# A fused RWKV-7 block loop on one core: the key's square moves to ScalarE, the decay less its step to VectorE, and two queues are reordered

## The reference, cut to what matters

```
w_log = -softplus(-(w0 + tanh(wd) @ w_lora_up)) - 0.5
decay = exp(-exp(w_log))
a  = sigmoid(a0 + ad @ a_lora_up)
kk = k * k_k
kk = kk * rsqrt(sum(kk*kk, per head) + 1e-12)
k  = k * (1 + (a - 1) * k_a)
S_t = S_{t-1} diag(decay_t) + (S_{t-1} (-kk_t)) (kk_t * a_t)^T + v_t k_t^T
y_t = S_t r_t
```

## Time and profile before

| what | value |
|---|---|
| median of 3 runs | 2628.68 us (2628.33 to 2629.49) |
| profiled execution | 2628.31 us, its span 2626.6 us |
| granted TensorE clock, mean | 0.988 |
| PE busy | 2547.5 us, 97% of the span |
| DVE busy | 1520.5 us, 58% |
| ACT busy | 1163.3 us, 44% |
| POOL busy | 484.0 us, 18% |

### The profile page before, as it was taken

The page is one execution under the profiler, slowest core; times in us unless marked ns, Lnnn a source line. Parts: engine busy times, 40 slices in busy tenths (PEclk is TensorE's granted clock), DMA queues, the critical chain, the costliest instruction groups (busy, mean ns, idle before and its releaser), DMA issues.

```text
span 2626.6 us, 74898 instructions
## 1 busy us (share of the span) xinstructions
PE 2547.5 (97%) x30741; PEld 2102.5 (80%) x30741; DVE 1520.5 (58%) x3199; ACT 1163.3 (44%) x2626; POOL 484.0 (18%) x622
## 2 busy tenths in 40 slices
PE   6999999999999999999999999999999999999995
PEld 6777777777778888888888888888888888888883
DVE  2412121212157677777767777776677777667774
ACT  3324242323225455544445554454455445445542
POOL 3210101010121112211211121121112112111210
PEclk8999999999999999999999999999999999999997
DMA  8632322323210001000000101000010100001000
GB/s 338 255 112 81 110 93 99 102 90 112 81 65 10 26 29 39 26 34 26 26 26 26 42 26 34 26 26 26 26 42 26 34 26 26 26 26 42 26 18 25
DMA packets 68706, 153.08 MB, mean 58 GB/s; under 512 B 3977, under 2 KB 37342, under 8 KB 66398
## 3 DMA queue, kind: packets, MB, share of 16 engines
q1 hardware_dynamic: 63134, 130.08, 14.1%
q0 software_dynamic: 1680, 11.01, 1.0%
q10 hardware_dynamic: 3632, 7.87, 0.8%
HBM read 98.61 MB, written 50.33 MB: 57 GB/s over the span
## 4 chain that ended last, share of the span: by engine, by line
PE 74%; DVE 16%; ACT 4%; issue 3%; DMA 1%; DVEq 0%; SPq 0%; ACTq 0%
PE banks L949 20%; PE banks L355 16%; PE banks L984 9%; PE banks L387 8%; PE banks L932 7%; PE banks L1004 6%; DVE SM L1587 2%; DVE LA L1570 2%; DVE LA L1576 2%; PE banks L960 1%; PE banks L1112 1%; DVE t L1467 1%; DVE mix L1438 1%; DVE kk L1474 1%; DVE stmp L1519 1%
## 5 line engine op out<-in xcount | busy, mean ns | idle before, releaser
L949 PE MATMUL banks<-xT,w 128*128 128x128 f32 x5232 | 634.0, 279 | 0.0
L949 PEld LDWEIGHTS banks<-xT,w 128*128 128x128 f32 x5232 | 598.3, 192 | 31.1 <-issue 27.1
L1255 ACT ACTIVATE LX<-banks 128x512 f32<-128x512 f32 (+1 forms) x384 | 184.9, 524 | 642.6 <-DVE WT L1532 436.5
L355 PE MATMUL banks<-xT,w 128*128 128x256 f32 x2048 | 448.3, 381 | 4.8 <-ACT xT L475 4.8
L355 PEld LDWEIGHTS banks<-xT,w 128*128 128x128 f32 x2048 | 391.3, 191 | 65.3 <-issue 10.5
L932 PE MATMUL banks<-xT,w 128*64 128x128 f32 x6944 | 420.1, 274 | 0.0
L932 PEld LDWEIGHTS banks<-xT,w 128*64 128x64 f32 x6944 | 380.3, 137 | 6.3
L984 PE MATMUL banks<-wo,Y 128*128 128x512 f32 x512 | 234.3, 601 | 4.7 <-DVE Y L1492 4.7
L387 PE MATMUL banks<-wo,yc 128*128 128x512 f32 x512 | 224.8, 592 | 0.0
L672 DVE TENSOR_SCALAR gate<-gate 128x1024 f32<-128x1024 f32 x16 | 11.1, 694 | 367.7 <-ACT gate L495 367.7
L1532 DVE TENSOR_TENSOR WT<-banks,level_mask 128x256 f32<-128x256 f32 x256 | 102.6, 422 | 187.7 <-PE banks L1004 179.7
(11 more groups left out here) (185 smaller groups left out, 3587.6 us busy)
## 6 DMA issues: line engine op xcount, KB each, us to landing
x_in<-in_x SPq DMA_DIRECT2D x16, 1024.0 KB, 7.4
xr<-in_x SPq DMA_DIRECT2D x32, 512.0 KB, 4.3
xt_dram<-xT SPq DMA_DIRECT2D x32, 512.0 KB, 8.6
h_dram<-xr SPq DMA_DIRECT2D x32, 512.0 KB, 2.6
xT<-xt_dram SPq DMA_DIRECT2D x32, 512.0 KB, 3.3
gate_row<-h_dram SPq DMA_DIRECT2D x32, 512.0 KB, 4.3
out<-gate_row SPq DMA_DIRECT2D x32, 512.0 KB, 2.6
w<-in_w_in POOLq DMA_DIRECT2D x8, 1088.0 KB, 10.9
```

The source lines that it names most:

```text
L355: last = nc.tensor.matmul(bank[t // 2][:, (t % 2) * T1:(t % 2 + 1) * T1], w1[:, k, t * P:(t + 1) * P], xT[:, k, :], start=(k == 0), stop=( ...
L949: last = (by_halves if halves else nc.tensor.matmul)(bank[b][:, q * P:(q + 1) * P], w2[:, k, (t0 + q) * P:(t0 + q + 1) * P], xT[par][:, k, :],
L1255: s(nc.scalar.activation(to, of, ACT.Copy), lx_ready, hold=False)
```

## The change

Four things change, in the steady blocks and, the first two, in the prologue too.

1. The key's square leaves POOL (L1368) and becomes an ACT instruction, `key_square`, with function Square. In a block it stands behind `sigmoid(0)`, which itself moves ahead of `second_values(SV)`.
2. The subtraction for `egx` leaves POOL (L1370) and becomes a DVE instruction, `decay_ahead`, behind `take_r(1)` and ahead of `new_key`.
3. `state_sum(j)` waits for `s_ps` instead of `y_ps`. The wait for `y_ps` moves to `new_state(0)` and, for the second chunk, to the start of the next `run`.
4. DVE's order: `clamp(1)` goes between `state_sum(0)` and `new_state(0)`; `decay_sum` ahead of `take_r(1)`; the first two instructions of `replaced_key` (now `taken_key`) ahead of `shift(3)`, its last two (`decayed_key`) stay behind. ACT's order: `sigmoid(1)` ahead of `key_scale`.

```diff
 ACT:
+                def key_square():
+                    hd.wait(kk_ready, 1)
+                    hd(nc.scalar.activation(rn[:, :, :], kk[:, :, :], ACT.Square), kk2_ready, hold=False)
...
                     if ahead:
                         exp_low_rank(1)
+                        sigmoid(0)
+                        key_square()
                     s.wait(y_ps, 1)
                     second_values(SV)
...
                     if ahead:
-                        sigmoid(0)
+                        sigmoid(1)
                         key_scale()
-                        sigmoid(1)
                     take_u(1)
 POOL:
-                    hd.wait(kk_ready, 1)
-                    hd(nc.gpsimd.tensor_tensor(rn[:, :, :], kk[:, :, :], kk[:, :, :], ALU.mult), kk2_ready)
-                    hd.wait(G_ready, 1)
-                    hd(nc.gpsimd.tensor_tensor(egx[:, :, :], G[:, :, :], sig[:, 0], ALU.subtract), gprev_ready)
 DVE:
+                def decay_ahead():
+                    hd(nc.vector.tensor_tensor(egx[:, :, :], G[:, :, :], sig[:, 0], ALU.subtract), gprev_ready, hold=False)
...
-                def replaced_key():
+                def taken_key():
                     hd.wait(rn_ready, 1)
                     hd(nc.vector.tensor_tensor(kk[:, :, :], kk[:, :, :], rn[:, :, :], ALU.mult))
                     hd(nc.vector.scalar_tensor_tensor(out=t2[:, :, :], in0=kk[:, :, :], scalar=-1.0, in1=sig[:, 1],
                                                       op0=ALU.mult, op1=ALU.mult))
+
+                def decayed_key():
                     hd.wait(exps_ready, 1)
...
                 def state_sum(j):
-                    s.wait(y_ps, j + 1)
+                    s.wait(s_ps, j + 1)
...
                     if not first:
                         pv.block(n - 1)
+                        pv.wait(y_ps, NC)
...
                     state_sum(0)
+                    if ahead:
+                        clamp(1)
+                    s.wait(y_ps, 1)
                     new_state(0, s, s_ready)
                     if ahead:
-                        clamp(1)
+                        decay_sum()
                     take_r(1)
                     if ahead:
-                        decay_sum()
+                        decay_ahead()
                         new_key()
                     state_sum(1)
                     if ahead:
+                        taken_key()
                         shift(n + 1, 3)
-                        replaced_key()
+                        decayed_key()
```

## The result

| kernel | median, us | runs | ratio to before, 95% |
|---|---|---|---|
| before | 2628.8 | 4, 2628.33 to 2629.49 | |
| changed | 2611.45 | 4, 2610.13 to 2612.34 | 0.9931 [0.9918, 0.9944] |

The change saves 17.3 us, 0.7%. The profiled execution took 2610.13 us, its span 2608.4.

The account below looks back on a forecast made before the run. TensorE sets the pace, with a link through VectorE once per block. From 2628.31 us, 31 x 0.45 = 14.0 and 0.9 (last block) go, 0.9 of stalls comes back: 2614.3, stated as 2614.5; range for 8 in 10, 2604 to 2624.

Parts of the forecast that it names:

- What TensorE could win: Its waits for VectorE's LA and W at block start: at most 0.91 us in A, 0.56 in B.
- g: How much earlier VectorE gets to LA and W, decided between clamp and BK: about 0.45 us a block.
- A: Block kind where TensorE waits for LA and again for W: 0.48 and 0.43 us to win.
- B: The other, alternating block kind: 0.42 us to win at the wait for LA, 0.14 at W.
- The 0.2 us for POOL's copy of prev's column: End of VectorE's sequence: this copy now meets VectorE's BK and takes back up to 0.2 us.
- The hold of kk and t by BK: Behind state_sum(1), POOL's BK holds up VectorE's kk and t: together 2.4 to 2.6 us instead of 1.4.
- The first rival: BK and taken_key miss each other, no hold-up: g 1.6, TensorE's limits bind, 2605 us; chance 0.12.
- the largest step: State_sum(1) starts behind L1058, at about 1858.1 against 1859.57, 1.47 us earlier, allowed by s_ps rather than y_ps.
- ScalarE in the middle: Ln, Exp, Square and SV copies end just in time for TensorE: stall 0 to 0.2 us a block, taken 0.03.
- The margin of 0.2 us: Mid-block, ahead of L1034: ScalarE could be about 0.2 us later before TensorE's 0.03 us stall starts to grow.
- The prologue: Egx fills VectorE's idle time, the square moves between idle engines: 0, plus or minus 1 us.
- The last block: TensorE waits 2.04 us for new_state(0); with state_sum(0) not waiting for y_ps, 0.9 us is saved.

Follow-up runs that it names:

- e3: Changed kernel with POOL making only a 64x64 piece of each half of BK in the blocks: 2603.9 us in one run.
- e9: Changed kernel with kk ahead of k2, t ahead of state_sum(1), rk behind it, and the square first in ScalarE's prologue: 2601.98 us, ratio 0.9894.
- e7: Kernel before the change, with state_sum waiting for s_ps and the waits for y_ps moved accordingly: 2626.53 us, ratio 0.9992.
- e1: Changed kernel with state_sum waiting for y_ps again in both chunks: 2639.1 us, ratio 1.0035.
- e10: Changed kernel with state_sum(1) alone waiting for y_ps, state_sum(0) still for s_ps: 2618.31 us in one run.
- e8: Changed kernel with the key's square back on POOL, in the blocks and the prologue: 2617.25 us in one run.
- e6: Changed kernel with a second Square of 128x512 on ScalarE ahead of the key's square in each block: 2625.31 us in one run.
- e2: Changed kernel with the key's square ahead of the eight exponentials in ScalarE's prologue: 2608.21 us in one run.
- e5: Changed kernel with kk and t ahead of state_sum(1), rk behind it, and the square first in ScalarE's prologue: 2605.34 us, ratio 0.9913.
- e4: Changed kernel with the last shift ahead of kk and t again: 2619.26 us, ratio 0.9961.

## Why the prediction was right

Direction and mechanism held: 2611.45 against 2614.5, inside the range of 2604 to 2624. But three terms were off, and they partly cancelled.

*What TensorE could win and g.* Right in kind: the wait for LA is gone, the one for W in A is partly left. The size was too small: 0.70 us in A and 0.76 in B instead of 0.45, 22.4 us instead of 14.0 (of the 31 blocks 16 are of kind A and 15 of kind B, not the other way round as I counted; this makes the first rival's 22.6 a 23.0 and touches no other sum). One part is g. From L1058 to VectorE's BK it is 5.42 us now (1846.81 to 1852.23) and was 6.09 (1857.35 to 1863.44), so g is 0.67 and not 0.45. The 0.2 us for POOL's copy of prev's column was the wrong item: it starts 0.05 us ahead of BK and takes 0.22, and BK takes 1.43 against 1.41, so it holds nothing up. The other part is that L1112 can follow L1103 after 0.52 us; I had read 0.62 from the profile, which hid 0.1 us of wait. With my limit of 0.56 in B, the g of 0.67 would have been cut short there; the real limit is 0.64 (0.51 at LA and 0.13 at W). The remaining 0.07 us a block came between L1034 and the variance (3.95 to 3.90 and 6.66 to 6.64), which no step of mine foresaw and no run isolated.

*The hold of kk and t by BK.* This was the step I was least sure of. Kk and t take 2.38 us from start to end (1848.47 to 1850.85), at the low end of the forecast's 2.4 to 2.6. e3 shows that POOL's BK is the cause, e9 that who is issued first decides who waits. The rule of the Trainium skill that I weighed (SBUF — State Buffer, "Who interferes with whom") agrees, also in what it exempts: in e9 state_sum and the shift, with one input in PSUM, take 0.88 and 1.12 us beside BK. Only the end of the hold differs a little from the rule's whole length: the way is free about 0.14 us ahead of BK's recorded end. The first rival is what e3 shows, 2603.9 against 2605, but its limits were too low: the pair is 113.44 where they gave 113.73 (115.20 less 0.91 and 0.56). The 31 blocks are 27.0 us shorter than before in e3 instead of 22.6, and the later start of the second pass (2.7) and a last block that gained 0.1 instead of 1.9 hide that in the time.

*State_sum(1) and s_ps.* It starts 0.1 us behind the end of L1058, as forecast. But I called it the largest step and said that s_ps allows it. That was wrong as a statement of cause. In the kernel before, VectorE reached state_sum(1) when rk was done (1859.53), later than y_ps, so s_ps alone changes nothing (e7). It counts only in the new order, and there it is needed in both chunks (e1, e10). That what made room for it is POOL's two instructions gone, the shorter clamp and L1472 and the earlier sigmoid(1) is read from the rows; only the square has a run of its own (e8). I had not priced state_sum(0) at all, where it is worth more, 1.01 us of the pair.

*ScalarE in the middle.* The square ended at 1841.92 where TensorE reads it at 1842.05, no stall, as forecast with 0.03. The margin of 0.2 us is e6's; I had placed it at L1034, and by e6 it is at the key's norm: what a late ScalarE delays first is the square itself.

*The prologue.* I said the square moves from one idle engine to another, 0 plus or minus 1. It cost 2.2 us (e2), and 3.8 where the clock fell behind the wait. ScalarE was idle, but its queue was not free: the square stood behind eight exponentials that wait for L960, and kk had been ready since 749. The key's norm is followed by 14 us of TensorE's products, all delayed.

*The last block.* The 0.9 us at new_state(0) came, and W's wait fell from 5.75 to 5.42 us. ScalarE's 2.3 us, which the profile puts on "issue", took more than that back. They come with the square on ScalarE (e8), so they are a cost of the change that I had put at nothing; why ScalarE stands still stays open. Another 0.5 us is an L984 that takes 5.44 us instead of 4.95, more of it at the lower granted clock. The same stretch in the other traces lies between 65.1 and 70.8 us: besides the idle time of ScalarE, single products there run now at one level of the clock and now at the other (the first L1034 takes 0.69 us before and 1.12 in the changed kernel, the variance 1.97 and 1.08).

In sum, against the forecast of the profiled execution (2614.3, measured 2610.13): the steady blocks gave 9.3 us more, the start of the second pass came 2.6 later (2.2 of it the prologue, the rest ahead of it), and the last block gave 2.4 less. So 5.0 of the 9.3 us cancel, and the forecast is as near as it is in part by luck.

## What to carry to other kernels

Take a wait's worth from what arrives last there, not from how much earlier the new signal is: s_ps was worth nothing in one order and over 20 us in the other. An instruction that moves to an idle engine moves into that engine's queue, so look at what stands ahead of it in every copy of the queue, the prologue's too, and look at the code that runs once: the steady blocks gained 13.2 us from the square's move, and its place in the prologue cost 2.2 or more and ScalarE's pause in the last block 2.3 (e2, e8). Where two engines hold each other up, it is enough to be issued first: 0.13 us of order was worth 1 us of VectorE's time, though only 0.17 us a pair of blocks in the whole (e5 and e9), because TensorE had little left to wait for.

## What the runs showed of the hardware

A VectorE instruction of 128x512 with both inputs in SBUF takes 0.69 us alone and 1.65 to 1.69 when a POOL instruction that reads SBUF was issued just ahead of it; one with an input in PSUM keeps its time beside the same POOL instruction (0.88 for two of 64x256, 1.12 for four of 128x128). A tensor_scalar of 128x512 goes from 0.43 to 1.27 when a POOL instruction of 1.04 was issued 0.06 us ahead of it. POOL is held the same way: the two halves of BK take 2.63 us when nothing meets them (e4), 2.98 when kk is issued ahead of the second (changed kernel), 3.39 when t is issued ahead of the first and rk ahead of the second (e9). The hold ends a little ahead of the POOL instruction's recorded end: in the changed kernel t ends at 1850.85, so, if its own 0.69 us are the last of it, they began at 1850.16, while BK's record ends at 1850.30.

A pause of TensorE of 2.78 us can cost more than itself: behind it the granted clock fell in four of seven traces, and the 32 products of L387 took 15.3 to 15.7 us instead of 14.0.
